# Softmax weights transposed by DMA instead of by the matrix engine, and value matmuls one unit pair later, in an eight-core hybrid decoder

## What is computed

```python
for l in range(2):
    x = x + 0.5 * swiglu(rms_norm(x, ffn1_norm[l]), ...)      # D 1024, D_FF 2816
    z = rms_norm(x, mix_norm[l]) @ w_in[l]                    # 1536 columns
    # A: scores = q k^T / 8 in blocks of 128 queries x 256 keys, 8 heads, 2 kv heads,
    #    masked to a band of 128; p = exp(scores - m); p = p / (sum(p) + exp(sink - m))
    #    y_attn = p @ v
    # B: gelu(u) * (tril(W_s) rms_norm(gelu(v)) + b), chunks of 128
    # C: causal means over 2/4/8/16 tokens minus the token, a small matmul, a scale
    x = x + concat(y_attn, y_gmlp, y_pool) @ w_out[l]
    x = x + 0.5 * swiglu(rms_norm(x, ffn2_norm[l]), ...)
return rms_norm(x, final_norm)
```

## Time and profile before

| | |
|---|---|
| median of 3 runs | 2548.74 us (2548.2 to 3018.87) |
| the profiled execution | 2550.56 us, its slowest core's span 2549.0 us |
| PE busy | 2411.7 us (95%) |
| DVE, ACT, POOL busy | 1450.7, 824.6, 440.7 us |
| DMA | 181.58 MB, mean 71 GB/s |

### The profile page before, as it was taken

How to read it: one execution, slowest core, us unless ns; L and a number is a source line. 1 busy time by engine, 2 the same in 40 slices (tenths; PEclk the granted TensorE clock), 3 DMA queues, 4 the chain that set the end, 5 groups by cost and what they waited for, 6 DMA issues and landing times.

```text
span 2549.0 us, 49305 instructions; the slowest of 8 cores (2544.5 to 2549.0 us)
## 1 busy us (share of the span) xinstructions
PE 2411.7 (95%) x16264; PEld 1547.7 (61%) x16264; DVE 1450.7 (57%) x3079; ACT 824.6 (32%) x1899; POOL 440.7 (17%) x641
## 2 busy tenths in 40 slices
PE   2699999999999999999999999999998999999994
PEld 0366656666656665666666666766665777666662
DVE  3533364885565986653336335587655698663335
ACT  3111135453144652311122113545313555331112
POOL 1000002440003431000000000143000344000000
PEclk9899999999999999999999999999999999999997
DMA  8144433433434343444444454442443444264442
GB/s 217 29 69 66 68 61 61 71 53 58 67 66 69 61 64 64 71 67 67 70 65 75 76 79 65 67 71 44 72 71 65 79 70 68 45 131 72 67 64 84
DMA packets 80085, 181.58 MB, mean 71 GB/s; under 512 B 6496, under 2 KB 51808, under 8 KB 79840
## 3 DMA queue, kind: packets, MB, share of 16 engines
q0 software_dynamic: 66784, 160.03, 39.8%
q1 hardware_dynamic: 13056, 18.41, 2.3%
HBM read 330.03 MB, written 8.39 MB: 133 GB/s over the span
## 4 chain that ended last, share of the span: by engine, by line
PE 89%; issue 3%; DVE 3%; DMA 2%; ACT 2%; SPq 0%; DVEq 0%; POOL 0%; ACTq 0%; POOLq 0%
PE PS L457 88%; DMA s_X<-xT 1%; DVE s_H L510 1%; PE PS L761 1%; DVE PS L508 1%; ACT L542 0%; ACT s_stm L542 0%; DVE s_aT L547 0%; DMA s_MW<-wout 0%; ACT s_sqb L501 0%; ACT PS L506 0%; ACT L506 0%; DVE s_stm L544 0%; DVE s_X L510 0%; DVE s_dT L708 0%
## 5 line engine op out<-in xcount | busy, mean ns | idle before, releaser
L457 PE MATMUL PS<-s_H,s_FW 128*128 128x384 bf16 (+1 forms) x8448 | 1349.9, 318 | 46.4 <-DVE s_aT L547 31.1
L457 PEld LDWEIGHTS PS<-s_H,s_FW 128*128 128x128 bf16 x8448 | 823.2, 98 | 517.3 <-issue 64.3
L457 PE MATMUL PS<-s_aT,s_FW 128*128 128x384 bf16 (+1 forms) x4224 | 685.2, 317 | 4.3 <-DVE s_X L560 4.1
L547 DVE TENSOR_TENSOR s_aT<-s_stm,PS 128x384 bf16<-128x384 f32 x528 | 278.2, 528 | 511.9 <-PE PS L457 507.8
L457 PEld LDWEIGHTS PS<-s_aT,s_FW 128*128 128x128 bf16 x4224 | 410.5, 98 | 236.0 <-issue 8.7
L560 DVE SCALAR_TENSOR_TENSOR s_X<-PS,s_X 128x384 f32<-128x384 f32 (+1 forms) x768 | 405.0, 532 | 198.2 <-PE PS L457 194.7
L539 ACT ACTIVATE s_stm<-PS 128x384 f32<-128x384 f32 (+1 forms) x264 | 127.2, 482 | 793.3 <-PE PS L457 762.4
L457 PE MATMUL PS<-s_H,s_MW 128*128 128x384 bf16 (+2 forms) x1632 | 257.3, 313 | 1.3 <-DMA s_MW<-wout 1.3
L567 POOL DMA_DIRECT2D s_FW<-wgu x176 | 96.2, 548 | 906.7 <-PE PS L457 874.7
L542 ACT ACTIVATE s_stm<-PS 128x384 f32<-128x384 f32 (+1 forms) x264 | 122.0, 465 | 346.7 <-PE PS L457 290.6
L573 POOL DMA_DIRECT2D s_FW<-wdn x128 | 91.9, 718 | 708.5 <-PE PS L457 662.1
(11 more groups left out here) (72 smaller groups left out, 1107.7 us busy)
## 6 DMA issues: line engine op xcount, KB each, us to landing
s_FW<-wgu POOLq DMA_DIRECT2D x176, 512.0 KB, 5.2
s_FW<-wdn POOLq DMA_DIRECT2D x64, 384.0 KB, 4.7
s_FW<-wdn POOLq DMA_DIRECT2D x64, 320.0 KB, 4.4
s_MW<-win POOLq DMA_DIRECT2D x24, 512.0 KB, 5.2
s_X<-xT SPq DMA_DIRECT2D x6, 1536.0 KB, 28.6
s_MW<-wout POOLq DMA_DIRECT2D x16, 512.0 KB, 5.6
out<-s_X SPq DMA_DIRECT2D x4, 1536.0 KB, 8.4
out<-s_X SPq DMA_DIRECT2D x2, 1024.0 KB, 12.6
```

Source lines behind the costliest of these rows:

```text
L457: return lambda e: e.matmul(out(), lhsT=lhsT(), rhs=rhs(), start=start, stop=stop)
L547: P.add("dve", [lambda e: e.tensor_tensor(out=aT[:, j, l0:l1], in0=stm[:, s.i, 0:NT], in1=fb(u)[:, 0:NT], op=ALU.mult)], t_dve(NT), rd=[s, ...
```

## The change

`unit` no longer transposes on PE. `Pm` is written in another order of its 512 columns, and one DMA on SP's queue, `dma_start_transpose`, turns the 128 x 512 tile in four 128 x 128 pieces into `PTs`, now four buffers of one unit each. The PSUM bank and the ACT copy of the transposes are gone. The value matmuls (`pv`) run for a pair of units (both `ty` of one `gi`), 256 columns wide, and are written one pair later: the pair's matmuls come after the scores of the next pair. The two pairs of a block share one PSUM bank `o`, held from the first pair's value matmuls until the copy after the second's; `gmlp(b)` follows that copy.

The planner changes too. Every pool now hands out its buffers strictly in the order in which the program first uses them (`order`, `turn`), for all classes; before, only class 1 held back, and only behind a task that was already available. The planner gives a transposing DMA 1.2 us of SP, 0.9 us of the queue and 3.9 us from start to landing.

```diff
@@ Prog.add @@
                 if not x.users:
                     t.opens.append(x)
+                    x.order = len(x.pool.queue)
+                    x.pool.queue.append(x)
@@ Prog.schedule @@
+            if any(h.i is None and h not in t.opens for h in t.handles):
+                return None
             count = {}
             for h in t.opens:
                 n = count.get(id(h.pool), 0)
+                if h.order != h.pool.turn + n:
+                    return None
                 count[id(h.pool)] = n + 1
...
-                blocked = set()
                 for t in avail[e]:
-                    if any(id(h.pool) in blocked for h in t.opens) and t.cls == 1:
-                        continue
                     r = ready_of(t)
-                    if t.opens and t.cls == 1:
-                        for h in t.opens:
-                            blocked.add(id(h.pool))
...
+                h.pool.turn += 1
...
-            if t.sem is not None:
+            if t.xpose:
+                x_free = max(x_free, s + 1.0) + 0.9
+                t.fin = x_free + 2.0
+            elif t.sem is not None:
@@ build_program @@
-        Pm = sb("Pm", [128, 2, 2, 256], BF16)
-        PTs = sb("PTs", [128, 1, 2, 2, 4, 128], BF16)
+        Pm = sb("Pm", [128, 2, 512], BF16)
+        PTs = sb("PTs", [128, 4, 4, 128], BF16)
...
-        pPTs = BufPool(1)
+        pPm.sems = [P.new_dma_sem() for _ in range(2)]
+        pPTs = BufPool(4)
@@ unit @@
-                P.add("pool", [lambda e: e.tensor_tensor(out=Pm[:, pm.i, :, :], in0=Eb[:, E.i, :, :],
-                                                         in1=sv(12).unsqueeze(2).broadcast_to([128, 2, 256]), op=ALU.mult)],
+                P.add("pool", [lambda e: e.tensor_tensor(out=Pm[:, pm.i, :].rearrange("p (k i j) -> p i k j", k=2, i=2),
+                                                         in0=Eb[:, E.i, :, :].rearrange("p i (k j) -> p i k j", k=2),
+                                                         in1=sv(12).unsqueeze(2).unsqueeze(3).broadcast_to([128, 2, 2, 128]), op=ALU.mult)],
                       t_pool(512), rd=[E, sm], wr=[pm])
-                tp = pG.new()
-                P.add("pe", [lambda e, i=i, kb=kb: e.transpose(gb(tp).bitcast(BF16)[:, (kb * 2 + i) * 128:(kb * 2 + i + 1) * 128],
-                                                               Pm[:, pm.i, i, kb * 128:(kb + 1) * 128], ident[:]) for i in range(2) for kb in range(2)],
-                      t_mm(*[128] * 4), rd=[pm, rcb], wr=[tp], lag=0.3)
-                P.add("act", [lambda e: e.activation(
-                    out=PTs[:, pt.i, ty, :, 2 * gi:2 * gi + 2, :].rearrange("p k c q -> p k (c q)"),
-                    in_=gb(tp).bitcast(BF16)[:, 0:512].rearrange("p (k c) -> p k c", k=2), func=AF.Copy)],
-                      t_act(512), rd=[tp], wr=[pt])
...
+                P.add("sp", [lambda e: e.dma_start_transpose(out=PTs[:, pt.i, :, :], in_=Pm[:, pm.i, :])], 1.2,
+                      rd=[pm], wr=[pt], sem=pm, xpose=True)
+
+            def pv(b, gi, pts, o):
+                P.add("pe", [mm(lambda: gb(o)[:, gi * 256:(gi + 1) * 256], lambda ty=ty, kb=kb: VP[:, b - base - 1 + kb, ty, :],
+                                lambda ty=ty, kb=kb: PTs[:, pts[ty].i, 2 * kb:2 * kb + 2, :].rearrange("p i q -> p (i q)"),
                                 ty == 0 and kb == 0, ty == 1 and kb == 1) for ty in range(2) for kb in range(2)],
...
+                if gi == 1:
...
+                    gmlp(b)
@@ mixer @@
+            late = []
             for b in range(ob0, zb1):
-                attn(b)
-                gmlp(b)
+                o = pG.new()
+                for gi in range(2):
+                    pts = []
+                    for ty in range(2):
+                        pts.append(pPTs.new())
+                        unit(b, ty, gi, pts[ty])
+                    late.append((b, gi, pts, o))
+                    if len(late) > 1:
+                        pv(*late.pop(0))
+            pv(*late.pop(0))
```

More of the change, by code:

```diff
@@ L51 @@
 class Handle:
-    __slots__ = ("pool", "i", "res", "users", "left")
+    __slots__ = ("pool", "i", "res", "users", "left", "order")
     def __init__(self, pool):
@@ L68, in __init__ @@
         self.sems = None
+        self.queue = []
+        self.turn = 0
     def new(self):
@@ L75 @@
     __slots__ = ("id", "eng", "instrs", "deps", "dur", "cls", "sem", "opens", "handles", "func",
-                 "start", "fin", "idx", "val", "nleft", "outs", "nbytes", "lag")
+                 "start", "fin", "idx", "val", "nleft", "outs", "nbytes", "lag", "xpose")
 class Prog:
@@ L88, in new_dma_sem, with add @@
         return self.n_dma_sem - 1
-    def add(self, eng, instrs, dur, rd=(), wr=(), func=None, sem=None, nbytes=0, cls=None, lag=0.0):
+    def add(self, eng, instrs, dur, rd=(), wr=(), func=None, sem=None, nbytes=0, cls=None, lag=0.0, xpose=False):
         t = Task()
@@ L95, in add @@
         t.lag = lag
+        t.xpose = xpose
         t.opens, t.handles = [], []
@@ L142, in schedule @@
         order = {e: [] for e in ENGS}
-        dma_free = 0.0
+        dma_free = x_free = 0.0
         table = None
@@ L218, in schedule @@
                     t.sem = h.pool.sems[bi]
+            if isinstance(t.sem, Handle):
+                t.sem = t.sem.pool.sems[t.sem.i]
             dur = t.dur
@@ L726, in pool_tile, with unit @@
                       t_act(no, 1), rd=[g, rc], wr=[r for b in range(o0, a1) for r in yr(b, 6 + c, 7 + c)])
-            def unit(b, ty, gi, pt, mk):
+            def unit(b, ty, gi, pt):
+                mk = masks[:, 256:512] if b == OWNB else masks[:, 0:256]
                 q0, q1 = (b - ob0) * 128, (b - ob0 + 1) * 128
@@ L769, in attn @@
-            def attn(b):
-                mk = masks[:, 256:512] if b == OWNB else masks[:, 0:256]
-                pt = pPTs.new()
-                for ty in range(2):
-                    for gi in range(2):
-                        unit(b, ty, gi, pt, mk)
-                o = pG.new()
-                P.add("pe", [mm(lambda: gb(o), lambda ty=ty, kb=kb: VP[:, b - base - 1 + kb, ty, :],
-                                lambda ty=ty, kb=kb: PTs[:, pt.i, ty, kb, :, :].rearrange("p c q -> p (c q)"),
-                                ty == 0 and kb == 0, ty == 1 and kb == 1) for ty in range(2) for kb in range(2)],
-                      t_mm(*[512] * 4), rd=[pt] + rs(rVP, b - base - 1, b - base), wr=[o], lag=0.3)
-                P.add("act", [lambda e: e.activation(out=H[:, 0:4, b * 128:(b + 1) * 128],
-                                                     in_=gb(o).rearrange("p (c q) -> p c q", c=4), func=AF.Copy)],
-                      t_act(512), rd=[o], wr=yr(b, 0, 4))
+                P.add("sp", [lambda e: e.dma_start_transpose(out=PTs[:, pt.i, :, :], in_=Pm[:, pm.i, :])], 1.2,
+                      rd=[pm], wr=[pt], sem=pm, xpose=True)
```

4 lines of the change are left out of this document (added).

## The result

The changed kernel takes 2570.51 us (median of 5 runs; 2549.16 for the kernel before beside it). The ratio is 1.0083, 95% interval 1.0063 to 1.0103: 21 us slower, where 17 us faster was predicted. That lies inside the range of 2508 to 2602, on its far side, and within 2% of no change.

A forecast was written before the change was run, and what follows sets the result against it. PE was taken to bound the kernel, busy 2411.7 of 2549.0 us; 2550.6 - 29.0 + 0.5 + 3 + 9 = 2534 us profiled, so 2532 for the median, with a range of 2508 to 2602 (8 in 10).

The forecast's parts named there:

- 29.0: Attention on PE: 528 transposing matmuls, in 132 fours of 0.22 us, leave PE, -29.0 us.
- The room: Attention blocks: time a transfer may take before PE's value matmuls wait, 4.3 to 6.1 us, taken as 5.5.
- One pause shortly before the last FFN: PE at the last mixer's end: one pause of 15 to 20 us, with DVE busy in L518 and L520.
- Rival C: Attention: value matmuls wait in every block, single queue sets the pace above 4.4 us a transfer; over 2600 us; chance 0.21.
- It fits; where a block is slower than the mean it will not quite, and I put 3 us in all there: Attention: a transfer of 5.0 us against room of 5.5 stays hidden, except 3 us in all in slower blocks.
- the part on the weight loads beside it: Attention: weight loads of 5.2 us, issued two or three chunks ahead, DMA engines 29% busy; effect nothing.
- The second pair has more: 15.4 us, but its weights are not held by a next pair's masks.: Attention block, second pair: 15.4 us of cover for its transfers, with no next pair's masks delaying its weights.
- rival B: Attention: the transfer is a little late in most blocks, 6.5 to 8 us against 5.5; 2558 to 2601 us; chance 0.22.
- Mixer starts: Norms after an FFN: PE idles less as reciprocals come one at a time, -8 us, bounds 0 and -14.
- End of the last mixer: Last mixer's end: PE idles 18 us where it idled 4.7, +13 us, bounds +8 and +20.
- The +4 for the ends of the two middle mixers: Ends of layer 0's second and layer 1's first mixer: norm lies among down projections, 2 us each.
- The page's price: Transposing DMA: 1309 ns per 128 x 128 piece, estimated 5.2 us a unit, 10.5 a pair, a wait in every block.

The follow-up runs named there:

- e1: The changed kernel without its 132 transposing transfers, value matmuls reading weights set to zero once, same order otherwise: 2520.9 us, ratio 0.9887.
- e3: The changed kernel with the FFN's weight loads after the first eight cut to a small part of a tile: 2515.3 us, ratio 0.9865.
- e2: The changed kernel with four buffers for the softmax weights between POOL and the transfers in place of two: 2552 us, ratio 1.0009.

## Why the prediction was wrong

The kernel was forecast to become 17 us faster and became 21 us slower, clear of the noise.

**What held.** Everything but the transfers came out near the sum: 2550 less 29.0 is 2521, and e1 took 2520.9. PE's busy time on core 0 fell from 2411.7 to 2385.6 us in e1, 26.1 where 29.0 had been priced; nothing points at a cost of the value matmuls or a gain from ACT's copies, though neither was run alone. The room was put at 5.5 us and measured at 5.2 and 5.5. One pause shortly before the last FFN was named with its lines; its window has 15.3 us without work, 11.8 of them in one piece, 18 predicted. The median landing, taken as 5.0 us, is even shorter, 3.9. Rival C's one mechanism, a queue that sets the pace at t above 4.4 us, didn't come: e3. (Its sums are slightly off: 4 x 5.2 is 20.8, not 20.9, so its 2625 is nearer 2622; and the load of 128 KB at 10.7 us was not the only one, the masks' took 13.7.)

**The step that failed** is "It fits; where a block is slower than the mean it will not quite, and I put 3 us in all there". It compares one number for the transfer with one number for the room. The transfers spread from 2.4 to 8.4 us, and PE waits for the later one of two in each pair. With a room of 5.2 to 5.5 us a third of the pairs (24 of 66) waited, 1.7 us on the mean. The term was 3 us and measured 49.6: 41.6 of waits on core 0, the rest a PE that is busier for the same work, mostly by a lower clock beside the pauses (up to 8.5 of 10.7 us). The prediction listed "a transfer whose time grows when weight loads run beside it" among what would make it wrong, but gave it neither a price nor a chance, and closed the part on the weight loads beside it with "Nothing". That was the wrong way round: I had asked what the transfers do to the loads (5.2 us before, 5.4 with transfers, 5.6 in e1 without any: nothing indeed) and not what the loads do to the transfers. DMA was 29% busy in the earlier trace rows and a load runs for 5.2 us of each 7.8, so most transfers had to meet one.

**A second omission.** "The second pair has more: 15.4 us, but its weights are not held by a next pair's masks." They are held by something else: two `Pm` buffers, free now only when a transfer has landed, where before it was PE's transposes that freed them. Of PE's 41.6 us 17.9 are for second pairs held so. e2 prices it at 18.5 us; e3 shows that it costs only where transfers are long.

**The size was rival B's, the mechanism not.** B's range of 2558 to 2601 holds the result. But B had transfers of 6.5 to 8 us late in most blocks; they have a median of 3.9 and are late in 24 of 66 pairs. The resemblance is one of sums.

**The planner's terms.** Mixer starts: -8 taken, about -14 measured, the bound given. End of the last mixer: +13 taken, about +10.6 measured. The +4 for the ends of the two middle mixers did not show (windows 1000 to 1650 on core 0 lost 3.6 us where 8.2 were lost before). Together +9 predicted, about 0 measured by e1 (which also holds whatever the 29.0 us were off). This error pulled towards the result: the transfers were 46.6 us worse than their term, and the forecast missed by only 38.

**The page's price.** The estimate from the Trainium skill ("VectorE: DVE Perf Modes", "The three transpose paths"), 5.2 us a unit, is neither the time alone (2.4 us) nor the median (3.9); its case, a wait in every block, did not come, and the trace does not agree with it.

## What to carry to other kernels

Where a wait has room, compare it with the spread of what it waits for, above all when the wait is for the later of two, and take the spread from transfers that run beside the kernel's other traffic: with a room 1.3 us over the median, a third of these pairs was still late. Look first at what is issued in the same moment: a weight load within 0.6 us of the second transfer went with a late pair in 144 of 166 cases. Moving the loads' issue away from the transfers is the remedy that these runs suggest and that none of them tried. When a consumer becomes a DMA, ask again for each buffer it reads what now frees it and who stands behind that. A planner that assumes the median of a transfer (3.9 us here) leaves its slower half to be waited for; 1.5 us more was worth 24 us here, after 8 us that went into longer mixers.

## What the runs showed of the hardware

- A transposing DMA of a 128 x 512 bf16 tile takes 1.19 us of SP's queue to issue and lands 2.4 us after the start of its issue when nothing else moves; it moves as 512 records of 256 bytes, of 0.018 us each. Several transfers can be in flight one behind the other.
- Beside a weight load of 512 KB it lands up to 8.4 us after its issue (core 0), in the median 0.5 us after a load that was issued before it; records of 1024 bytes in place of 4096 in the load change nothing of that. No cost to the load shows: its median landing, taken core by core, is 5.15 to 5.65 us with the transfers and 5.08 to 5.88 without (e1).
- Short pauses on PE, of some 2 us each, go with a lower granted clock: 0.97 over the 200 us with 19.9 us of pauses, 1.00 over those with 3.1. With six waits of 2.0 to 3.3 us on core 0 went a short stretch at the lower of the two levels. PE's busy time there was 10.7 us longer than without transfers, for the same instructions.
- The cores lie further apart with the transfers: spans of 2552.6 to 2565.6 us against 2544.5 to 2549.0 before, and 2515.1 to 2519.1 without transfers.
